# Two transformer blocks on one core: a pipelined mLSTM pass, tokens in the weight queue, sums read a tile early, and a shared-expert block moved behind the first experts' products

## The reference, cut to what matters

```
block 1, layer 0: hgrn2 (4 heads) and mLSTM (4 heads, both directions), then a swiglu over 2816
block 1, layer 1: attention (8 heads, 2 kv heads), then a swiglu
block 2, layer 0: gated short convolution, then hier_moe
block 2, layer 1: gated delta net (8 heads), then hier_moe
hier_moe: top-1 group of 8, top-2 experts of its 8; 64 experts of 1024 -> 256 -> 1024, gated;
          plus sigmoid(x @ w_sg) * swiglu_shared(x), the shared expert having width 512
mLSTM weight of key s for query t: q_t.k_s * exp(-max(rowmax_t - col_s, 0)), masked to s <= t
          (direction 0) or s >= t (direction 1) inside a 128-block; out = weights @ [v, 1], normalised
```

## Time and profile before

| | |
|---|---|
| median of 3 runs | 2932.03 us (2928.23 to 2935.8) |
| profiled execution | 2935.02 us, its span 2933.2 us |
| mean granted TensorE clock | 0.939 of full |
| PE / DVE / ACT / POOL busy | 85% / 29% / 15% / 7% of the span |
| moved by DMA | 722.16 MB, mean 246 GB/s |

### The profile page before, as it was taken

How to read it: one execution, slowest core, us unless ns; L and a number is a source line. 1 busy time by engine, 2 the same in 40 slices (tenths; PEclk the granted TensorE clock), 3 DMA queues, 4 the chain that set the end, 5 groups by cost and what they waited for, 6 DMA issues and landing times.

```text
span 2933.2 us, 33956 instructions
## 1 busy us (share of the span) xinstructions
PE 2494.8 (85%) x13698; PEld 1342.9 (46%) x13698; DVE 844.3 (29%) x1770; ACT 436.3 (15%) x810; POOL 203.1 (7%) x267
## 2 busy tenths in 40 slices
PE   5998996799999998899989877767699988777676
PEld 3454555444444445444476433333277854323222
DVE  3155638510120036400033311111157652111011
ACT  1032221110010012200010100000123421000001
POOL 3122111110010011010010100000000020000000
PEclk8999998899999999999999998888889989989888
DMA  6676578244445353144663799999941357999997
GB/s 247 213 240 249 204 253 301 94 165 157 144 165 171 129 168 122 68 161 151 219 193 128 309 414 415 415 421 416 363 134 55 92 207 305 412 408 419 421 407 292
DMA packets 265449, 722.16 MB, mean 246 GB/s; under 512 B 15312, under 2 KB 149104, under 8 KB 211952
## 3 DMA queue, kind: packets, MB, share of 16 engines
q1 hardware_dynamic: 251808, 690.00, 62.2%
q0 software_dynamic: 13520, 30.41, 3.1%
HBM read 719.17 MB, written 1.18 MB: 246 GB/s over the span
## 4 chain that ended last, share of the span: by engine, by line
PE 68%; DMA 19%; DVE 7%; SPq 2%; ACT 2%; issue 2%; POOL 0%; DVEq 0%; ACTq 0%; POOLq 0%
PE ps L914 24%; DMA ring<-in_moe_w_up 16%; PE ps L1530 10%; PE ps L1027 8%; PE ps L939 5%; PE ps L1129 4%; PE ps L1111 3%; SPq L561 2%; PE ps L1083 2%; PE ps L1647 2%; PE ps L950 1%; PE ps L919 1%; DMA ring<-in_ada_w 1%; PE ps L1303 1%; PE ps L1518 1%
## 5 line engine op out<-in xcount | busy, mean ns | idle before, releaser
L914 PE MATMUL ps<-ring,hT 128*128 128x512 f32 x1632 | 724.9, 598 | 17.7 <-ACT hT L1774 12.2
L914 PEld LDWEIGHTS ps<-ring,hT 128*128 128x128 f32 x1632 | 308.5, 192 | 385.3 <-issue 366.9
L1530 PE MATMUL ps<-arena 128*32 128x512 f32 x1536 | 283.9, 716 | 153.4 <-DMA ring<-in_moe_w_up 149.5
L1530 PE MATMUL ps<-ring,arena 128*32 128x512 f32 x512 | 283.1, 716 | 0.0
L1027 PE MATMUL ps<-ring,arena 128*128 128x512 f32 x528 | 232.2, 592 | 2.4 <-ACT arena L1855 2.4
L1530 PEld LDWEIGHTS ps<-arena 128*32 128x32 f32 x1536 | 72.2, 127 | 338.9 <-issue 235.4
L2361 DVE SCALAR_TENSOR_TENSOR arena<-ps,arena 128x256 f32<-128x256 f32 x66 | 28.0, 425 | 578.9 <-ACT arena L1851 578.7
L939 PE MATMUL ps<-hT,ring 128*128 128x256 f32 x768 | 174.7, 390 | 2.5 <-ACT hT L1774 1.5
L939 PEld LDWEIGHTS ps<-hT,ring 128*128 128x128 f32 x768 | 150.0, 197 | 25.0 <-ACT hT L1774 2.3
L1027 PEld LDWEIGHTS ps<-ring,arena 128*128 128x128 f32 x528 | 100.1, 190 | 127.7 <-issue 127.7
L1553 PE MATMUL ps<-ring,arena 128*32 128x512 f32 x1024 | 131.3, 658 | 22.1 <-ACT arena L2146 21.3
(11 more groups left out here) (543 smaller groups left out, 2434.8 us busy)
## 6 DMA issues: line engine op xcount, KB each, us to landing
ring<-in_moe_w_down SPq DMA_DIRECT2D x128, 1024.0 KB, 17.0
ring<-in_ada_w SPq DMA_DIRECT2D x48, 2048.0 KB, 12.5
arena<-in_moe_w_gate SPq DMA_DIRECT2D x96, 1024.0 KB, 11.3
arena<-in_moe_w_up SPq DMA_DIRECT2D x96, 1024.0 KB, 9.7
ring<-in_ffn_w_in SPq DMA_DIRECT2D x66, 1024.0 KB, 8.8
ring<-in_ffn_w_out SPq DMA_DIRECT2D x33, 1024.0 KB, 5.0
ring<-in_moe_w_gate SPq DMA_DIRECT2D x32, 1024.0 KB, 15.6
ring<-in_moe_w_up SPq DMA_DIRECT2D x32, 1024.0 KB, 17.6
```

Source lines behind the costliest of these rows:

```text
L914: m = pe.matmul(o3, lhsT_of(k), ring[:, a:a + 2, k * EH:(k + 1) * EH], start=start and k == 0, stop=stop and k == KC - 1)
L1530: m = pe.matmul(ps[a * CAP:(a + 1) * CAP, 6, :].rearrange("p (u c) -> p u c", u=2), x_slots[:, k, a * CAP:(a + 1) * CAP], slot_pair(gate_s ...
```

## The change

**Beginning**: `ctx` and `x` are issued by SP, `ctx` behind the third conditioning group and `x` behind the fourth; squares and roots are made for two tiles at a time, behind `ada_rows`; each group is spread right behind its product. **mLSTM pass**: `p_sb` is doubled, the row maxima run two passes ahead, ACT does the `max` as a Relu with bias and then the exponentials, only the columns that a direction sees are computed, one masked product covers four diagonal blocks, and DVE weights pass i+1 before it waits for the sums of pass i. `ada_rows` stands behind the small sums (in pass 0 behind the wait for `out_g`). **Sums**: `update_tile` of tile 0 starts when that tile's sums are there, after the last feed-forward and both experts' stages; the product with zeros goes. **Experts**: the weights of the shared expert's second half get a place of their own, of which one half is `v_scale` and `v_shift`; its product for tile 1 moves behind the gates and ups of quad 0; the fourth expert's gate and up and two downs are issued earlier; the first half's weights use slots 4 and 5 in both layers (in the convolution layer these still hold `conv_out_w`; 1 and 2 before did not). The shared down quarters run in quads 1, 2, 3 and 3. POOL's `post()` behind each expert opening, and in the first the `pre()` behind it, wait for the second quad's gates and ups. The next four down loads wait for two scatter products where they waited for one.

```diff
-        arena = sb("arena", [P, ARENA])
+        ARENA = 24248
+        arena = sb("arena", [P, ARENA + 2 * D])
+        v_scale, v_shift = arena[:, ARENA:ARENA + D], arena[:, ARENA + D:ARENA + 2 * D]
+        shared_second = arena[:, ARENA - UNIT:ARENA + UNIT].rearrange("p (u n) -> p u n", u=2)
...
         o_ml = A(4, NT)
-        p_sb = A(4, NT)
+        p_at = A.at
...
         h_routed = [hT[:, :, t * P:(t + 1) * P] for t in range(2)]
 
...
+        def seen_by(si, d):
+
+            return slice(si * P, NT) if d == 0 else slice(0 if si < 2 else SEQ, NT if si < 2 else (si + 1) * P)
+
+        def scores_of(si, cols):
+
+            return ps[:, si, cols] if si < 2 else ps[:, 2, slice(cols.start - SEQ * (3 - si), cols.stop - SEQ * (3 - si))]
...
-                for i in range(2):
-                    for part in range(2):
-                        fill(SHARED_SLOT[l][i][part], shared[i][part])
-                    if i == 0 and ahead is not None:
-                        ahead()
-                early = [a for a in (0, 3) if DOWN_SLOT[a] not in SHARED_SLOT[l][0]]
-                for a in early:
+                for part in range(2):
+                    fill(SHARED_SLOT[part], shared[0][part])
+                if ahead is not None:
+                    ahead()
+                fill(GATE_SLOT[0][3], kmajor(I["moe_w_gate_2"][l, 3]))
+                fill(UP_SLOT[3], kmajor(I["moe_w_up_2"][l, 3]))
+                for a in range(2):
                     fill(DOWN_SLOT[a], I["moe_w_down_2"][l, a].rearrange("(p j) n -> p (j n)", j=2))
                 n.block += 4
                 sp.wait_ge(block_done, b0 + 1)
+                for part in range(2):
+                    sp.dma_start(shared_second[:, part, :].rearrange("p (k n) -> p k n", k=KC), shared[1][part]) \
+                        .then_inc(sem("shared_second_loaded"), 16)
                 for i in range(2):
                     wd = I["shared_w_down_2"][l][i * EH:(i + 1) * EH, :].rearrange("(p j) n -> p j n", j=2)
                     for j in range(2):
                         sp.dma_start(SHARED_DOWN[i][j], wd[:, j, :]).then_inc(sem("shared_down_loaded"), 16)
-                used_gate_up, used_down = sem("quad_gate_up_used"), sem("quad_down_used")
+                used_gate_up, used_down = sem("quad_gate_up_used"), sem("tile_0_scattered")
 
...
                 sp.wait_ge(block_done, b0 + 2)
-                gate_up_load(GATE_SLOT[0][3], I["moe_w_gate_2"][l, 3])
-                gate_up_load(UP_SLOT[3], I["moe_w_up_2"][l, 3])
-                for a in (0, 3):
-                    if a not in early:
-                        down_load(DOWN_SLOT[a], I["moe_w_down_2"][l, a])
-                sp.wait_ge(block_done, b0 + 4)
-                down_load(DOWN_SLOT[1], I["moe_w_down_2"][l, 1])
-                down_load(DOWN_SLOT[2], I["moe_w_down_2"][l, 2])
+                for a in range(2, QUAD):
+                    down_load(DOWN_SLOT[a], I["moe_w_down_2"][l, a])
...
-                n.block += 1
                 n.pos = 0
                 sp.wait_ge(used_gate_up, QUADS * (l + 1))
                 for s in range(SLOTS):
-                    free_at[s] = n.block if s in DOWN_SLOT else 0
-
-            ada_groups(FIRST_GROUPS)
+                    free_at[s] = 0
+
+            def tokens(i, src):
+                sp.dma_start(x_sb[:, 2 * i:2 * i + 2, :], src.rearrange("(t p) d -> p t d", p=P)).then_inc(tokens_loaded[i], 16)
+
+            ada_groups(FIRST_GROUPS - 1)
+            tokens(0, I["ctx"][0])
+            ada_groups(1)
+            tokens(1, I["x"][0])
...
+                if j == DOWN_SLOT[0]:
+                    sp.wait_ge(sem("tile_0_scattered"), QUADS)
...
             n.h += 2
+            pool.wait_ge(sem("quad_gate_up_used"), 2)
...
+                        if tile_told and t == 0:
+                            m.then_inc(sem("first_sums_complete"), 1)
...
-            for g in range(2):
+            for g in range(4):
                 ada_groups(1, FIRST_BANK[g])
-            pe.wait_ge(constants_loaded, 48)
-            for g in range(4):
-                if g < 2:
-                    ada_groups(1, FIRST_BANK[g + 2])
+                if g == 0:
+                    pe.wait_ge(constants_loaded, 48)
...
+
+            def head_scores(hd):
                 q0 = 64 * (hd % 2)
                 qh, kh = qk[q0:q0 + 64, hd // 2, :], qk[q0:q0 + 64, 2 + hd // 2, :]
-                if hd >= 1:
-                    pe.wait_ge(sem("ml_weights"), 8 * hd)
                 for si in range(4):
                     c0 = 0 if si < 2 else SEQ
...
+            def row_max(i):
+                row = 32 * (i % 2) + i // 2
+                pe.matmul(ps[:, 4 + i % 2, :], ident[0:ROWS, row:row + 1].broadcast_to([ROWS, P]), rows_d,
+                          start=True, stop=True).then_inc(sem("ml_max"), 1)
+
+            row_max(0)
+            row_max(1)
+            head_scores(0)
+            pe.wait_ge(tp_evacuated, n.tp)
+            for hd in range(MLSTM_HEADS):
                 for d in range(2):
                     i = 2 * hd + d
                     pe.wait_ge(sem("ada_rows_ready"), ada_next[0])
-                    if i >= 2:
-                        pe.wait_ge(sem("ml_weights"), 4 * (i - 1))
-                    row = 32 * d + hd
-                    pe.matmul(ps[:, 4 + d, :], ident[0:ROWS, row:row + 1].broadcast_to([ROWS, P]), rows_d,
-                              start=True, stop=True).then_inc(sem("ml_max"), 1)
-                    ada_groups(ADA_B[i], 5 - d)
+                    ada_groups(ADA_B[i], 3)
                     if i == 0:
...
+                    if i + 2 < 2 * MLSTM_HEADS:
+                        row_max(i + 2)
+                    if d == 1 and hd + 1 < MLSTM_HEADS:
+                        head_scores(hd + 1)
                     if i >= 1:
...
+            def shared_second_products(t, chunks):
+
+                for k in chunks:
+                    m = pe.matmul(ps[:, 4 + t, :].rearrange("p (u c) -> p u c", u=2), hT[:, k, SEQ + t * P:SEQ + (t + 1) * P],
+                                  shared_second[:, :, k * EH:(k + 1) * EH], start=k == 0, stop=k == KC - 1)
+                return m
...
                 pe.matmul(ps[:, 7, 128:192], ones_t[:, :], picked[:, 1, :], start=False, stop=True).then_inc(sem("ranks_summed"), 1)
-                shared_gate_up(l, 1, 0, gu0 + 1)
-                shared_turn(0, gu0 + 2)
+                pe.wait_ge(gu_evacuated, gu0 + 1)
+                pe.wait_ge(sem("shared_second_loaded"), 32 * (l + 1))
+                shared_second_products(0, range(0, KC // 2))
                 pe.wait_ge(sem("rounds_known"), l + 1)
                 rounds = pe.value_load(rounds_i[0:1, 0:1], min_val=1, max_val=SEQ // CAP)
+                shared_second_products(0, range(KC // 2, KC)).then_inc(block_done, 1)
+                shared_turn(0, gu0 + 2)
                 pe.wait_ge(sem("sums_opened"), 4 * (l + 1))
                 pe.wait_ge(tp_evacuated, tp0 + 1)
...
+                    if second:
+                        shared_second_products(1, range(KC)).then_inc(block_done, 1)
+                    for part in meanwhile:
+                        shared_down(l, *part)
                     pe.wait_ge(S("quad_hid"), c + 1)
...
+                        if second and half == 1:
+                            pe.wait_ge(gu_evacuated, gu0 + 4)
...
+                            m.then_inc(S(f"tile_{t}_scattered"), 1)
 
                 filled0 = list(used)
...
-                    one_round(rounds * (q + 1) + before - 1, q % 2, landed, True, first=q == 0, turn=q == 0, meanwhile=divmod(q, 2))
+                    one_round(rounds * (q + 1) + before - 1, q % 2, landed, True, first=q == 0, second=q == 0, turn=q == 1,
+                              meanwhile=[(), [(0, 0)], [(0, 1)], [(1, 0), (1, 1)]][q])
...
                             with pe.Fori(1, rounds) as r:
                                 one_round(q * rounds + before + r - 1, parity, landed)
...
                 nc.scalar.preload_act_table(ACT.Sqrt)
                 for i in range(2):
-                    update_tile(i, complete)
+                    wait_for_sums(i)
+                    update_tile(i, None)
+
+            def feed_forward_sums(i):
+                act.wait_ge(block_done, n.block) if i == 1 else act.wait_ge(sem("first_sums_complete"), 1)
...
+            for i in range(2):
+                act.wait_ge(sem("mean_square"), i + 1)
+                tell(nc.scalar.activation(stat[:, 1, 2 * i:2 * i + 2], stat[:, 0, 2 * i:2 * i + 2], ACT.Sqrt, scale=1.0 / D, bias=eps_t[:, :]),
+                     sem("rms_ready"))
+            n.normed = 2
...
             for i in range(8):
+                hd, d = divmod(i, 2)
+                row = 32 * d + hd
...
+                    act.wait_ge(sem("ml_out"), i - 1)
                 for si in range(4):
-                    k = 4 * i + si
-                    act.wait_ge(sem("ml_gap"), k + 1)
```

(52 more changed lines are left out.)

183 lines of the change are left out of this document (92 added, 91 removed).

## The result

The changed kernel takes 2911.2 us in the median of 4 runs (2904.6 to 2913.3), the one before 2933.0; the ratio is 0.9923, interval 0.9902 to 0.9945. In a second series it takes 2911.2 again (6 runs, 2900.5 to 2918.3) against 2938.8, ratio 0.9903, interval 0.9878 to 0.9929. So it is 22 to 28 us faster where I forecast 33.

What follows compares the result with a forecast made beforehand. It took DMA to bound the beginning and quads, a loop the mLSTM pass, and predecessors the rest. Gains of 5.5, 22, 2.8, 5.2, 4.0 and 8.2 less costs of 9.8 and 4 gave -33.9; forecast 2899 us, range 2880 to 2912.

Steps and rivals of the forecast that it cites:

- third rival: Experts: second half's weights land late, stream loses the opening's gain, layers even or worse by 8 in all; 2915, chance 0.10.
- held loop: mLSTM loop held by PE near its low clock and POOL's stores; gain only 12 us, 2909, chance 0.16.
- Beginning: Kernel start: tokens in SP's order bring the first turn of a token tile 5.5 us earlier, at 42.8.
- mLSTM: mLSTM passes: PE's sum overlaps DVE's weighting of the next pass; gain 22 us, bounds 12 and 30.
- price of the Relu: mLSTM passes: four Relus on ACT take at most 2.2 us of its 4.4 a pass, hidden.
- Early sums: Last feed-forward and both experts' ends: ACT starts on tile 0's sums sooner; gains 2.8, 2.6 and 2.6 us.
- Openings: Expert openings: PE's tile 1 block leaves the path to the first quad; gains 4.0 and 8.2 us.
- late weights: Convolution layer's opening: first half's weights wait for slots held by `conv_out_w`, land at 1609.6, 4.2 us late.
- land as the ranks are done: Expert openings: second half's weights need 7.5 us and land as the ranks are done; 2 us late delays all behind.
- Quads: Experts' quads: vectors in the stream and late PE cost 9.0 us in the first layer, 4.8 in the second.
- vectors' 1.4 us each: Quads: vectors now load inside the full stream; two such loads took 2.78 us, seven cost 9.8.
- 2 of lost stream a layer: Quads: moved work makes PE 5 us late, part comes back; 2 us lost a layer, 4 together, bounds 0 and 8.

Runs made afterwards that it cites:

- ten profiles: Profiles of the changed kernel (two) and of eight kernels that leave the mLSTM passes alone; passes 0 to 3 take 43.0 to 52.4 us.
- half the bytes: Changed kernel with half the weights of 13 mLSTM conditioning groups left out, results wrong, run once; passes 0 to 3 take 37.0 us.
- first profile: Profiled run of the changed kernel in its first series, the fastest of four, 6.6 us below their median of 2911.2 us.
- The slots alone: Changed kernel with the shared expert's first half in free ring places 1 and 2 in the convolution layer; median 2904.1 us, ratio 0.9894 to the kernel before.
- second profile: Profiled run of the changed kernel repeated with no edit in a second series; median of 6 runs 2911.2 us, ratio 0.9903 to the kernel before.

## Why the prediction was right, and where its sizes were off

The range holds the time, but narrowly, and the reason is not that every term was right. The mLSTM stage, the early sums and the beginning came in the size that I had worked out. The experts did not: by the table above they cost 4.9 and 6.7 us in all, early sums apart, where I had forecast 1.6. That is in part my third rival (the second half's weights late, the quads' stream losing what the opening gained, 8 worse in all, 2915), whose time is nearer to the measured 2911 than my 2899 is. The time alone would also fit the held loop (2909), but that rival had a gain of 12 in the mLSTM stage, and no profile of these passes has less than 19. That the shortfall stayed inside the range is some luck.

**Beginning** (5.5; 5.7 to 6.0). The fourth group lands where I put it (31.55). Two steps were off against each other: the spread takes 2.05 us, not 3.2, and the squares of `x`, which I had hidden behind it, end behind it, so the scale starts 0.8 late, at 38.43. (The terms that I gave add up to 42.5, not to 42.8.) The reason was half wrong: only 2.2 to 2.5 us hang on the tokens' queue.

**mLSTM** (22; 19 to 26 in ten profiles, mean 23). Size right, mechanism wrong in half of the passes. I had worked a loop between VectorE and PE for all eight and wrote of the weights that they do not decide, from their landing for the last group alone. Between sum 0 and sum 4 PE does eight groups, two a pass: 4.2 MB at the 388 GB/s that I had used are 10.8 us a pass, 43 for four. 43.0 is the shortest that any profile with all bytes has, and half the bytes shortens exactly these. The sums are 6.3 to 14.1 us apart in the first profile where I had expected 8 to 11 for the normalisations. The price of the Relu (2.2 of 4.4 a pass) was 1.8 to 1.9. The rival of a loop held by PE at its low clock was true in part: at 0.79 passes 0 to 3 take 6 us more than at 0.96. The rule of the Trainium skill (ScalarE: Activation LUTs, Rules for kernel authors) that max and Relu belong on VectorE is not borne out here: 1.89 against 1.92 us for the set, and 4.9 us lost, in part to the clock, when VectorE, the full engine of passes 4 to 7, does it. The factor of up to three that the page gives is for bf16, and these operations are float32. The same page says (Table sets) that Relu is in every table set; this trace agrees, for it has one load of 1.28 us ahead of the first exponentials, at 423.45, and the next, for the square root, at 490.14, with seven sets of Relus and eight of exponentials between.

**Early sums** (2.8, 2.6, 2.6; 2.7, 2.6, 2.6). Right, and the steadiest terms of all.

**Openings** (4.0 and 8.2; 1.3 and 7.1 to 10.5). The late weights were seen (4.2; 4.6 measured), but two things behind them were not: the first half's product, started after that idle time, is stretched to 9.7 us up to the next turn from 8.4, and PE waits 1.4 to 1.7 for the second half's weights, which I had as "land as the ranks are done". The slots alone give back 5.8, the wait and the stretching together.

**Quads** (-9.0 and -4.8; -11 and -6). The vectors' 1.4 us each was right in the second layer (3.0 for two). The failing size is "2 of lost stream a layer": it is 5.0 and 3.6 by the stretch (11.3 and 6.1 longer) less the 2.62 and 1.05 MB that POOL's queue carried in it, at 416 GB/s. In the second layer all of it, and in the first 3 us, lie in quad 3, where I had counted the second quarter but let it come back in the shorter next product. It does come back in part (28.7 to 28.8 for the next step, 29.2 and 29.7 before), after the stream had run dry. The rest in the first layer is a gap at the start of quad 1 that is not the same in every profile; why is not shown.

**What I had at nothing**: the attention layer, whose code is the same, and which has 4.4 of the 6.8 us that the table shows lost up to the last feed-forward, 3.5 of the 4.6 in the second profile. From the end of the feed-forward ahead of it to its mixer it took 138.1 us before and 141.2 to 142.4 in eleven of the thirteen profiles behind, at a granted clock of 0.94 or 0.95 instead of 0.99; with 0.96 it took 140.0, with 0.99 138.4. The first profile's:

```profile
1047.10:1189.53 142.43, 119.94 (x464) 73.32 (x464) 72.48 (x145) 40.19 (x85) 17.30 (x13) 0.94 0.26 84
```

PE is busy 4.6 us longer there for the same products, so it is the clock that takes these 3.5 to 4.4 us; what decides whether it dips stays open, and with one profile of the kernel before it is not shown that the change brings it. The delta layer was 2.5 to 4 us faster in the same way, at 0.96 instead of 0.95. Such terms are what separates the profiles' sums from the medians, and the forecast was made against a single profile.

## What to carry to other kernels

Where a loop is tightened, compute for every pass what each queue must carry in it, not only for the last: the transfer that had room before is the next bound. A wait in front of a saturated stream is worth its full length, so look which buffers the first loads of such a stage go into; work moved into the stream is free only in those steps where the engine waits for weights, so look at each step by itself. And read the gain of an edit between two fixed rows of the profile, but learn first how well that stretch repeats: here the ends of stages repeat to 0.02 us, the quads' first five steps only to 5 and the first mLSTM passes to 9.

## What the runs showed of the hardware

With the DMA engines full and PE waiting for single weights, PE's granted clock over some 45 us of short bursts is 0.79 to 0.96 from one execution to the next of the same code; with half the bytes it was 1.00, in one execution. In the attention stage, whose code no kernel touches, the same products took 138.1 to 142.4 us at granted clocks from 0.99 to 0.94. Behind quads 0, 1 and 3, before and after the change, PE sits idle for up to 3.6 us ahead of its next gathers with no wait that the profile shows (2.7 to 3.0 before), but not behind quad 2; what it waits for stays open. In the changed kernel the gathers behind quad 3 then take 6.5 us from 2537.97 where others take 3.8. Four Relus of float32 out of PSUM with a bias take as long on ScalarE (1.89 us) as on VectorE (1.92).
